# A two-part transformer block on one core: where block 1 is turned and rounded among the products of a stage, and what the first product of the MLA's output waits for

## The reference, cut to what matters

```
for i in range(2):
    x = post_norm(x, 0.5 * swiglu_2(x, ffn1_w_in[i], ffn1_w_out[i]), ...)      # FFN c, FFN e
    mix = fox_mixer(...) if i < 1 else mla_mixer(...)                          # layer 1: MLA, 16 heads
    x = post_norm(x, mix, ...)
    x = post_norm(x, 0.5 * swiglu_2(x, ffn2_w_in[i], ffn2_w_out[i]), ...)      # FFN d, FFN f
    gate = sigmoid(x @ ple_w_gate[i] + ple_b_gate[i])                          # the gate of layer i
    x = post_norm(x, gate * (p[i] @ ple_w_proj[i]), ...)
```

## Time and profile before

| | us |
|---|---|
| median of 3 runs (lowest, highest) | 1739.42 (1739.07, 1739.47) |
| span of the profiled execution, first to last instruction | 1736.7 |
| TensorE matmul busy | 1674.9 (96%) |
| VectorE busy | 1185.4 (68%) |
| ScalarE busy | 873.0 (50%) |
| GpSimd busy | 76.0 (4%) |

### The profile page before, as it was taken

One profiled execution on the slowest core, in us unless ns is written; L12 is line 12 of the kernel. 1 busy time (PEld: TensorE's weight loads), 2 busy tenths in 40 slices (PEclk: granted clock), 3 DMA queues, 4 the chain that ended last, 5 costly groups with the idle time before them and its releaser, 6 DMA issues.

```text
span 1736.7 us, 24477 instructions
## 1 busy us (share of the span) xinstructions
PE 1674.9 (96%) x9836; PEld 1450.7 (84%) x9836; DVE 1185.4 (68%) x1949; ACT 873.0 (50%) x1497; POOL 76.0 (4%) x115
## 2 busy tenths in 40 slices
PE   7999999999999999999999999989999999999997
PEld 6888798888888888888878888778889887888885
DVE  5666646966666776675877667766667675576676
ACT  4544455655444544445655444544445565454444
POOL 0000002201000000001200000000000000100000
PEclk9999999899999999999999999999999999999999
DMA  8545255024555455445436554545445333455541
GB/s 347 190 182 186 107 201 237 1 97 170 185 194 199 174 208 192 182 146 219 146 146 229 198 196 171 193 174 185 182 176 203 117 113 119 162 222 200 189 158 49
DMA packets 32113, 301.57 MB, mean 174 GB/s; under 512 B 3824, under 2 KB 4352, under 8 KB 6016
## 3 DMA queue, kind: packets, MB, share of 16 engines
q1 hardware_dynamic: 32000, 300.01, 46.6%
HBM read 298.93 MB, written 1.06 MB: 173 GB/s over the span
## 4 chain that ended last, share of the span: by engine, by line
PE 86%; DVE 7%; ACT 5%; issue 1%; POOL 0%; DMA 0%; SPq 0%; DVEq 0%; ACTq 0%
PE bank L462 29%; PE bank L452 26%; PE bank L451 11%; PE bank L441 8%; DVE w_lo L414 3%; PE bank L454 2%; ACT w_hi L407 1%; PE bank L589 1%; PE bank L492 1%; PE bank L1155 1%; PE bank L1106 1%; DVE xT L849 1%; PE bank L1123 0%; DVE x L819 0%; ACT bank L721 0%
## 5 line engine op out<-in xcount | busy, mean ns | idle before, releaser
L414 DVE TENSOR_TENSOR w_lo<-w_raw,w_hi 128x1024 fp32r<-128x1024 f32 (+5 forms) x535 | 593.9, 1159 | 215.0 <-ACT w_hi L407 214.3
L452 PE MATMUL bank<-xT,w_hi 128*128 128x512 f32 x1920 | 674.2, 396 | 0.6 <-DVE w_lo L414 0.6
L407 ACT ACTIVATE w_hi<-w_raw 128x1024 fp32r<-128x1024 f32 (+5 forms) x543 | 507.9, 995 | 115.6 <-PE bank L462 93.5
L451 PE MATMUL bank<-xT,w_lo 128*128 128x256 f32 x1680 | 468.5, 279 | 0.0
L452 PEld LDWEIGHTS bank<-xT,w_hi 128*128 128x128 f32 x1920 | 351.8, 188 | 70.4 <-DVE w_lo L414 1.0
L451 PEld LDWEIGHTS bank<-xT,w_lo 128*128 128x128 f32 x1680 | 316.9, 189 | 10.5
L767 ACT ACTIVATE ff_silu<-ff_silu 128x256 f32<-128x256 f32 x123 | 51.5, 419 | 390.6 <-DVE ff_silu L917 390.6
L462 PE MATMUL bank<-w_hi,hT_hi 128*128 128x512 f32 x488 | 190.6, 391 | 0.5 <-DVE hT_lo L926 0.5
L462 PE MATMUL bank<-w_hi,hT_lo 128*128 128x512 f32 x488 | 189.9, 389 | 0.0
L462 PE MATMUL bank<-w_lo,hT_hi 128*128 128x512 f32 x488 | 189.9, 389 | 0.0
L917 DVE TENSOR_REDUCE ff_silu<-bank 128x256 f32<-128x512 f32 x123 | 84.9, 690 | 106.5 <-PE bank L452 105.1
(11 more groups left out here) (388 smaller groups left out, 2221.3 us busy)
## 6 DMA issues: line engine op xcount, KB each, us to landing
w_raw<-in_ffn_a SPq DMA_DIRECT2D x22, 1536.0 KB, 6.7
w_raw<-in_ffn_b SPq DMA_DIRECT2D x22, 1536.0 KB, 6.5
w_raw<-in_ffn_c SPq DMA_DIRECT2D x22, 1536.0 KB, 6.5
w_raw<-in_ffn_d SPq DMA_DIRECT2D x22, 1536.0 KB, 6.5
w_raw<-in_ffn_e SPq DMA_DIRECT2D x22, 1536.0 KB, 6.4
w_raw<-in_ffn_f SPq DMA_DIRECT2D x22, 1536.0 KB, 6.3
gains<-in_gains SPq DMA_DIRECT2D x11, 1024.0 KB, 4.8
w_raw<-in_mla_up SPq DMA_DIRECT2D x8, 1280.0 KB, 5.7
```

The costliest lines, as they stand in the source:

```text
L407: nc.scalar.activation(hi, src, ACTF.Copy).then_inc(w_hi_made, 1)
L414: nc.vector.tensor_tensor(lo, src, hi.bitcast(F32), ALU.subtract).then_inc(w_lo_made, 1)
L451: nc.tensor.matmul(o[:, 0:SEQ], lo[:, c], xT[:, k, 0, :], start=False, stop=False)
L452: ins = nc.tensor.matmul(o, hi[:, c], xT[:, k, :, :], start=(k == 0), stop=(k == KD - 1))
```

## The change

It moves waits and orders; the products, their operands and their number stay, but for six small TensorE instructions.

1. FFN c, d, e: `first_tile(b)` becomes `first_products(b, j, ks)`, so that tile j and a range of k can be asked for. Piece 2 is turned ahead of the last four k of block 0's second tile; piece 3 ahead of block 1's products.
2. FFN e (n = 7) alone: ahead of piece 2 a wait for the fourth sigmoid of the gate, and six 128x128 matmuls of the identity into bank 3.
3. The gates: block 1 is turned between the two halves of turn (0,0), with the wait for `proj_kept` that went with it.
4. Norm 7, block 1: ScalarE makes the high parts of pieces 0 and 1 between the two sigmoids; VectorE makes their low parts between the two adds.
5. MLA's output: turn (0,0) waits for 46 copies; 48 are waited for behind the step ahead of (0,1).

```diff
-            def first_tile(b):
+            def first_products(b, j, ks):
...
-                for j, o in enumerate(ff_banks(f, 0)):
-                    both = o.rearrange("p (two s) -> p two s", two=2)[:, :, tok_of(b)]
-                    for k in range(KD):
+                o = ff_banks(f, 0)[j]
+                both = o.rearrange("p (two s) -> p two s", two=2)[:, :, tok_of(b)]
+                for k in ks:
...
                     if n != 7:
                         pe_turn(n, src, (0, 1))
-                    first_tile(0)
-                    pe_turn(n, src, (2, 3))
-                    first_tile(1).then_inc(gate_up_made, 1)
+                    front, back = range(KD // 2), range(KD // 2, KD)
+                    first_products(0, 0, range(KD))
+                    first_products(0, 1, front)
+                    if n == 7:
+                        pe.wait_ge(gate_made, 4)
+                        for _ in range(6):
+                            nc.tensor.matmul(psum[3][:, 0:P], ident, ident, start=True, stop=True)
+                    pe_turn(n, src, (2,))
+                    first_products(0, 1, back)
+                    pe_turn(n, src, (3,))
+                    first_products(1, 0, range(KD))
+                    first_products(1, 1, range(KD)).then_inc(gate_up_made, 1)
...
                 if (c, b) == (0, 0):
-                    pe.wait_ge(mla_copied, 3 * MLA_H)
+                    pe.wait_ge(mla_copied, 3 * MLA_H - 2)
                 elif c < 2 and (c, b) != (0, 0):
                     step(MLA_H - 4 + 2 * c + b)
+                    pe.wait_ge(mla_copied, 3 * MLA_H)
...
+                if (c, b, half) == (0, 0, 1):
+                    pe.wait_ge(proj_kept, 4 * layer + 4)
+                    pe_turn(n, x, (2, 3))
                 if half:
                     return
...
                 elif (c, b) == (0, 1):
-                    pe.wait_ge(proj_kept, 4 * layer + 4)
-                    pe_turn(n, x, (2, 3))
                     pe.wait_ge(xT_lo_made, 4 * n + 3)
...
             act_ple_sigmoid(0, 0)
             act_squares(7, x, True, (0,))
-            act_ple_sigmoid(0, 1)
+            act_ple_sigmoid(0, 1, (0,))
             act_turn(7, (0, 1))
+            act_ple_sigmoid(0, 1, (1,))
             act_squares(7, x, True, (1,))
...
             def add_gated(layer, n, b):
-                dve_ple_add(layer, n, b)
+                dve_ple_add(layer, n, b, (0,))
+                if b and n == 7:
+                    dve_lows(n, 0)
+                dve_ple_add(layer, n, b, (1,))
                 dve_minus_mean(n, b)
...
-            dve_norm_blocks(7, lambda b: add_gated(0, 7, b), second=lambda: dve_lows(7, 0))
+            dve_norm_blocks(7, lambda b: add_gated(0, 7, b))
```

More of the change, by code:

```diff
@@ L581, in first_tile @@
                 wait_split(pe, at, 0, GU)
-                for j, o in enumerate(ff_banks(f, 0)):
-                    both = o.rearrange("p (two s) -> p two s", two=2)[:, :, tok_of(b)]
-                    for k in range(KD):
[L585 to L591, removed]
+                o = ff_banks(f, 0)[j]
+                both = o.rearrange("p (two s) -> p two s", two=2)[:, :, tok_of(b)]
+                for k in ks:
+                    pe.wait_ge(xT_lo_made, 4 * n + 2 * b + 1 + k // 4)
+                    w = slice((2 * k + j) * P, (2 * k + j + 1) * P)
+                    if k:
+                        nc.tensor.matmul(o[:, tok_of(b)], lo[:, w], xT[:, k, 0, tok_of(b)], start=False, stop=False)
+                    ins = nc.tensor.matmul(both, hi[:, w], xT[:, k, :, tok_of(b)], start=(k == 0), stop=(k == KD - 1))
+                    if k == 0:
+                        nc.tensor.matmul(o[:, tok_of(b)], lo[:, w], xT[:, k, 0, tok_of(b)], start=False, stop=False)
                 return ins
@@ L2259, in act_ple_gate, with act_ple_sigmoid @@
             act_split(first[f"ple{layer}_g2"])
-        def act_ple_sigmoid(layer, b):
-            for half in range(2):
+        def act_ple_sigmoid(layer, b, halves=range(2)):
+            for half in halves:
                 act.wait_ge(acc_made, 4 * PLE_NORM[layer] + 2 * b + half + 1)
@@ L2287, in dve_ple_gate, with dve_ple_add @@
             dve_split(first[f"ple{layer}_g2"])
-        def dve_ple_add(layer, n, b):
+        def dve_ple_add(layer, n, b, halves=range(2)):
             e = ple[layer]
-            for half in range(2):
+            for half in halves:
                 c = half_of(half)
```

## The result

Median 1728.00 us (five runs, 1726.05 to 1728.99) against 1739.07 (five runs, 1735.53 to 1739.47): ratio 0.9941, interval 0.9931 to 0.9952, so 8.3 to 12.0 us less. The profiled execution's own time was 1726.05, its span 1724.7.

A forecast was written before the change was run, and what follows sets the result against it. TensorE, busy 96% of the span, bounds the kernel; its idle or low-clock time counts. Terms -0.36 - 0.27 + 4.7 + 0.97 + 0.97 + 2.27 = 8.3, less 1.0 for the clock: 7.3, from 1739.42 to 1732.1 us, range 1730.0 to 1735.0.

The forecast's parts named there:

- The norm limit in FFN c and d: Piece 2's turn can begin only 0.81 us after VectorE's apply begins, so FFN c loses 0.36 us and d 0.27.
- Norm 7 with FFN e: Low parts moved into VectorE's idle stretch let FFN e's products start earlier: 4.7 us won at full clock.
- The MLA: At the MLA's output the 2.63 us gap ahead of turn (0,0) goes, 2.27 us won.
- rival (b): The MLA's win is taken back in turns (1,0) to (2,0): 2.27 us lost, 1734.4 us; chance 0.07.
- Rival (c): Norm 7: block 0's first products still come behind block 1's chain, 4.7 shrinks to 0.4, 1735.7 us; chance 0.05.
- rival (d): Slower: the new gap in FFN e brings the clock down and it stays down through the tiles; chance 0.02.
- the six small matmuls: In FFN e, 0.13 us each, ending at 1134.8 inside idle time and leaving TensorE idle 2.2 us.
- Rival (a): The clock stays up in FFN e: 8.3 us won, 1731.1 us; chance 0.34.
- the gap nearest in length: FFN e's 2.2 us idle stretch judged by the mixer's 2.42 us gap: clock falls 1.3 us after restart.
- the gates: Turning block 1 between the halves of (0,0) removes a 0.97 us gap in each gate: +0.97 twice.
- lying around the span: The 2.7 us between the median 1739.42 and the profiled span 1736.7, kept as time outside the span.
- the clock not lost: The forecast charged 1.0 us for the lowered clock behind FFN e's new gap, ends 0 and 4.0.

The follow-up runs named there:

- norm7_old_order: Changed kernel with ScalarE's and VectorE's old orders at norm 7 put back, TensorE's order staying as changed; single run 1734.34 us.
- mla_alone: Kernel before with only the waits at the MLA's output changed; single run 1735.59 us.
- three_small: Changed kernel with three instead of six small matmuls ahead of piece 2 in FFN e; that stage 15.76 us against 14.89, no whole-kernel time given.
- gates_alone: Kernel before with only block 1 of both gates turned between the halves of turn (0,0); single run 1737.28 us.
- again_after_2: Changed kernel, unedited, a third execution's profile; 1727.68 us.
- no_six: Changed kernel without the six small matmuls in FFN e, the wait for the fourth sigmoid kept, profiled twice; 1729.03 us, ratio 0.9947.
- cd_as_before: Changed kernel with FFN c and d given back the old order, pieces 2 and 3 turned together behind block 0's products; 1725.81 us, ratio 0.9928.
- one_k_back: Changed kernel with piece 2 turned ahead of only the last k of block 0's second tile in FFN c, d, e; 1727.37 us, ratio 0.9941.

## Why the prediction was right and wrong

**Right, by the profiles.** The norm limit in FFN c and d: the turn starts 0.81 us behind the apply (592.77 to 593.58), and c and d lose 0.33 and 0.25 (forecast 0.36 and 0.27). The waits behind this sum are listed shorter than forecast: 0.59 and 0.50 for the apply instead of 0.8 and 0.7, 0.17 (FFN c) and 0.18 (FFN e) for piece 3 instead of 0.5. A bracket begins at a modelled end; from start to start piece 3's step in FFN e takes 0.51 us (1136.01 to 1136.52), the same step elsewhere 0.17. Norm 7 with FFN e: 4.76 (4.7), with the low parts in VectorE's idle stretch; *norm7_old_order* shows that this is what brings it. The MLA: 2.25 (2.27), with chunk 1's split late next; rival (b) is out, for *mla_alone* still has 2.19 behind the wait for chunk 2's split (L1607 at 1468.61, 23.98 us from the column's first instruction, against 26.17 before). Rival (c) is out by the 1127.19 of L589, rival (d) by every profile.

**The step that failed: the six small matmuls at 0.13 us each.** They were priced by the transposes, "as eight transposes take 1.04". But each of the six stands as two records in the trace and takes 0.25 us (the row of L608: x12, 1.50 / 6), where a transpose stands as one and takes 0.13 (x8, 1.04). The trace of before had a row for the same instruction, which was not read: three of it in `pe_warm` (L482), two records and 0.28 us (0.83 / 3) each, shown as

```profile
1505.17 0.83 PE L482 MATMUL bank<-const 128*128 128x128 f32 x6
```

With 0.25 each the six end 0.7 us later (1.50 - 0.78), and the idle stretch is 1.5 us and not 2.2, far from the two gaps that the prediction weighed (2.42 and 2.63). Rival (a), "the clock stays up", is what three profiles show. How the clock answers to 2.2 us the forecast had right: *three_small* made that gap, had 0.50 for 3.4 us behind it and paid 0.87. The forecast's 0.45 us lost per us is that of a granted clock of 0.50 (22 products in 4.70 us, which take 2.6 at 1.00); 3.4 of it less 0.5 gave the 1.0. But to choose by "the gap nearest in length" stood on thinner ground than it seemed: the trace of before has two shorter gaps with a low clock behind them which were not read, 1.76 us at 23.49 and 0.40 with 1.17 at 1351.81. So 1.5 us would not have settled the matter from that trace alone. And the clock is not the whole miss: at no price for it the forecast was 1731.1, still above the range's lower end and 3.1 above what was measured.

**A term mis-sized: the gates.** 1.25 and 1.30 came, 0.97 and 0.97 were forecast with 1.0 as the end. The 0.97 us in brackets begin at the end that the profile models for the transposes (1109.34 + 1.03). From start to start a turn took 2.01 us in the old place and takes 0.79 in the new one (1104.65 to 1105.44), since nothing waits there: 2.01 - 0.79 = 1.22, and *gates_alone* has 1.22. The prediction had the 2.01 itself, and then took the bracket.

**The base.** The sum was laid against 1739.42, three runs that agreed within 0.4 us. Seventeen runs have 1738.34: 1.1 us of the miss. The 2.7 us "lying around the span" were in truth 1.3 to 1.4 around it and the rest the difference between one execution and the median. The range was built from the costs alone and had no room for what differs between executions ahead of the first changed instruction: *start* lies between 587.82 and 591.11 in five profiles, 1.8 us of it up to A and 1.5 for the clock behind the 1.75 us gap.

Together: forecast 7.3 won; the clock not lost +1.0, the gates +0.61, FFN c, d, e and MLA +0.09: 9.0, the ledger's sum. The medians differ by 10.7 us (1738.34 and 1727.62). Of the 1.7 between them up to 0.8 can be the MLA's gap, if before loses its clock there as often as the four profiles did; its own two don't show it. The rest is no more than *start* moves by itself, lies inside the interval of the ratio (7.8 to 12.3 us), and wasn't told apart.

Left open: why the clock holds in some executions and falls in others behind the same gap; in which share of all executions it does behind 2.63 us (four profiles are few); whether 1.54 us always keep it (six profiles of six, and 17 of 17 behind B's 1.55); and what makes the first 18 us differ.

## What to carry to other kernels

Price an instruction by a row of the same kind and type, and count its records: filler that is twice as long as thought turned the case here. Read a moved stall from start to start of the instructions around it, since the bracket begins at a modelled end. Before a forecast to a few tenths of a per cent, ask how far one kernel's executions lie apart: here one gap of TensorE, 1.75 us long, cost nothing in eleven profiles and 1.5 us in six, and what a gap costs in some executions is also what its removal saves in them. When executions differ, compare the time between fixed instructions stage by stage before naming a cause: a low average clock in one stage need not be where the time went (in the mixer 0.55 in after against 0.82 in *again_after_2*, and 0.6 us between them from C to *start*).

## What the runs showed of the hardware

- The granted clock after the same gap is not the same in each execution (1.75 us: 6 of 17 low; 2.63 us: 2 of 4), and the gap's length does not settle it (low behind 0.87 with 0.74 us, at 1.00 behind 1.55). "Fell" is from 1.00 to 0.50. Of the 17 profiles, for these gaps:

| gap, us | where | clock fell |
|---|---|---|
| 3.11 | mixer, C | 17 of 17 |
| 2.98 | FFN e, no_six, no_six_2 | 2 of 2 |
| 2.63, 2.64 | the MLA's output | 2 of 4, once ahead of the restart |
| 2.34 to 2.43 | mixer, the place of the earlier trace rows, where the clock was up before | 4 of 4 |
| 2.23 | FFN e, three_small | 1 of 1 |
| 1.96, 2.52, 2.52 | mixer, a later place (L1147 in gates_alone; again_after_2, cd_as_before) | 3 of 3 |
| 1.61 to 1.83 | mixer, this later place and that of the earlier trace rows | 0 of 12 |
| 1.75, 1.76 | at 21.6 to 23.5 us | 6 of 17 |
| 1.54 to 1.56 | FFN e | 0 of 6 |
| 1.55, 1.56 | at B | 0 of 17 |
| 0.40, then 1.17 | the MLA's start | 7 of 17 |
| 0.87, then 0.74 | FFN e, one_k_back | 1 of 1 |

- The small matmul of the float32 identity by itself, 128x128, stands as two records, a transpose as one. At a granted clock of 1.00 six small ones (L608 in after) take 1.50 us, 0.25 each, where eight transposes (1142.26 in before) take 1.04, 0.13 each. Each further one adds 0.22 ((1.50 - 0.83) / 3, from *three_small*). The program's first ten take longer at a reading of 1.00 too: 4.00 us in after, 4.64 in *again_after_2*.
- The first 18 us of the program differ by up to 1.9 us between executions (A at 16.30 in *three_small*, at 18.20 in before). No run here shows the cause: the granted clock reads 1.00 there in both. 1.9 us are 0.1% of 1728, but a quarter of the 7.3 us that was forecast.
